# Six stores in place of four for the rows of a 96-slot expert job

## The reference, cut to what matters

```
for e in range(N_EXP):
    out = out + combine[..., e:e + 1] * swiglu(h, w_gate[e], w_up[e], w_down[e])
h = h + out
return rms_norm(h, final_norm)
```

## Time and profile before

| | |
|---|---|
| median of three runs | 1287.35 us (1285.57 to 1287.72) |
| the profiled execution's own time | 1288.18 us |
| its span, first to last instruction | 1286.3 us |
| PE busy | 1225.8 us (95%) |
| DVE, ACT, POOL busy | 354.1, 298.1, 54.5 us |
| mean granted TensorE clock | 0.978 of full speed |
| DMA moved | 433.32 MB, mean 337 GB/s |

### The profile page before, as it was taken

One profiled execution on the slowest core, in us unless ns is written; L12 is line 12 of the kernel. 1 busy time (PEld: TensorE's weight loads), 2 busy tenths in 40 slices (PEclk: granted clock), 3 DMA queues, 4 the chain that ended last, 5 costly groups with the idle time before them and its releaser, 6 DMA issues.

```text
span 1286.3 us, 23777 instructions
## 1 busy us (share of the span) xinstructions
PE 1225.8 (95%) x10720; PEld 671.6 (52%) x10720; DVE 354.1 (28%) x758; ACT 298.1 (23%) x539; POOL 54.5 (4%) x99
## 2 busy tenths in 40 slices
PE   9999999999999999999999999999999989999827
PEld 9888888888887634234334233533443423443213
DVE  6787655557578501001001000100100100110013
ACT  7575644335566300000000000000000000000011
POOL 2012000000220300000000000000000000000010
PEclk9999999999999999999998999999999999999858
DMA  9534965545522999999999999999999999999980
GB/s 344 200 99 135 317 232 182 179 163 199 193 91 70 409 433 427 432 429 428 428 430 430 430 431 429 430 427 430 428 387 427 432 427 433 428 427 429 430 364 34
DMA packets 55045, 433.32 MB, mean 337 GB/s; under 512 B 3758, under 2 KB 8544, under 8 KB 41888
## 3 DMA queue, kind: packets, MB, share of 16 engines
q1 hardware_dynamic: 50416, 420.92, 79.7%
q0 software_dynamic: 2768, 8.52, 2.2%
q10 hardware_dynamic: 1760, 2.36, 0.5%
HBM read 423.26 MB, written 8.52 MB: 336 GB/s over the span
## 4 chain that ended last, share of the span: by engine, by line
PE 79%; DMA 14%; another core or an unknown queue 4%; DVE 2%; ACT 0%; issue 0%; SPq 0%; DVEq 0%; ACTq 0%
PE bank L2527 44%; PE bank L1900 9%; PE bank L1905 8%; PE bank L1901 8%; DMA ring<-in_od_w_gate_e_dram 6%; DMA aside<-in_od_w_gate_e_dram 3%; DMA ring<-in_od_w_down_e_dram 3%; DMA ring<-in_od_w_up_e_dram 2%; PE bank L2504 2%; PE bank L2616 1%; PE bank L2096 1%; PE bank L2177 1%; PE bank L2168 1%; PE bank L2367 0%; PE bank L2153 0%
## 5 line engine op out<-in xcount | busy, mean ns | idle before, releaser
L2527 PE MATMUL bank<-ring,xg 128*32 128x448 f32 x4128 | 398.8, 546 | 14.3 <-DMA ring<-in_od_w_up_e_dram 10.1
L2527 PEld LDWEIGHTS bank<-ring,xg 128*32 128x32 f32 x4128 | 133.5, 111 | 276.8 <-issue 254.5
L2527 PE MATMUL bank<-ring,m_ht 128*32 128x512 f32 (+1 forms) x2520 | 212.1, 497 | 7.8 <-DMA ring<-in_od_w_down_e_dram 7.8
L1819 DVE TENSOR_TENSOR m_hh<-m_hh,bank 128x896 f32<-128x896 f32 x20 | 21.7, 1087 | 619.1 <-PE bank L2527 618.9
L2527 PEld LDWEIGHTS bank<-ring,m_ht 128*32 128x32 f32 x2520 | 82.7, 111 | 133.5 <-issue 95.2
L1900 PE MATMUL bank<-w_hi,xt_hi 128*128 128x512 f32 (+3 forms) x384 | 147.1, 387 | 0.0
L1901 PE MATMUL bank<-w_hi,xt_lo 128*128 128x512 f32 (+3 forms) x384 | 142.9, 377 | 0.0
L1154 DVE TENSOR_TENSOR w_lo<-raw,w_hi 128x2048 fp32r<-128x2048 f32 (+4 forms) x52 | 114.6, 2211 | 44.2 <-ACT w_hi L556 43.2
L556 ACT ACTIVATE w_hi<-raw 128x2048 fp32r<-128x2048 f32 (+4 forms) x52 | 96.6, 1863 | 73.6 <-PE bank L1905 73.3
L2527 PE MATMUL bank<-aside,xg 128*32 128x448 f32 x992 | 97.1, 547 | 2.8 <-DMA aside<-in_od_w_up_e_dram 2.3
L1905 PE MATMUL bank<-w_lo,xt_hi 128*128 128x512 f32 (+3 forms) x384 | 91.9, 378 | 0.1
(11 more groups left out here) (358 smaller groups left out, 984.8 us busy)
## 6 DMA issues: line engine op xcount, KB each, us to landing
ring<-in_od_w_up_e_dram SPq DMA_DIRECT2D x26, 3584.0 KB, 25.3
ring<-in_od_w_down_e_dram SPq DMA_DIRECT2D x26, 3584.0 KB, 31.6
ring<-in_od_w_gate_e_dram SPq DMA_DIRECT2D x22, 3584.0 KB, 25.1
aside<-in_od_w_up_e_dram SPq DMA_DIRECT2D x6, 3584.0 KB, 25.1
aside<-in_od_w_gate_e_dram SPq DMA_DIRECT2D x6, 3584.0 KB, 32.8
aside<-in_od_w_down_e_dram SPq DMA_DIRECT2D x5, 3584.0 KB, 30.9
ring<-in_od_w_gate_e_dram SPq DMA_DIRECT2D x8, 1792.0 KB, 10.1
raw<-in_od_w_qkv_dram SPq DMA_DIRECT2D x12, 1024.0 KB, 5.1
```

What stands on the lines that cost most here:

```text
L1819: dve.tensor_tensor(halves(k), halves(k), both(up_bank(k)), ALU.mult).then_inc(m_h[k], 1)
L2527: return pe.matmul(B[bank][32 * g:32 * g + 32, c0:c0 + w.shape[-1]], tokens, w, start=first, stop=last, tile_position=(0, 32 * g))
```

## The change

A 96-slot job stores rows 0 to 31 and rows 64 to 95 by one store for each group of 32 partitions, four in place of two. So such a job has six stores, a 64-slot job still has four. The stores no longer add the same number to `y_stored`; `stores_before` gives how much the jobs before add, and the waits and the starting value follow from it. The wait of line 950, the release of the read-back and all other code stay as they were. (`big_before(j)` counts the 96-slot jobs before job j.)

```diff
+def stores_before(j):
+
+    return 96 * big_before(j) + 64 * (j - big_before(j)) if isinstance(j, int) else 96 * j - 32 * (len(SMALL_JOBS) - 1)
...
                 if last:
-                    act.wait_ge(y_stored, j * 64 + 64)
+                    act.wait_ge(y_stored, stores_before(j) + 96)
                     act.activation(stat[:, 92:93], ones[:, 0:1], ACT.Copy).then_inc(rows_all_stored, 1)
...
             def leave(j, thirds=ALL_THIRDS):
 
-                act.wait_ge(y_stored, j * 64 + 64)
+                act.wait_ge(y_stored, stores_before(j) + 96)
...
                     act.dma_start(to[:, 0:512], y[0:96, 0:512]).then_inc(y_stored, 16)
                     act.dma_start(to[32:64, 512:], y[96:P, 0:512]).then_inc(y_stored, 16)
-                    for k in range(2):
-                        act.dma_start(to[64 * k:64 * k + 32, 512:].rearrange("r (h f) -> h r f", h=2),
-                                      y[64 * k:64 * k + 64, 512:768]).then_inc(y_stored, 16)
+                    for g in range(4):
+                        r, c0 = 64 * (g // 2), 512 + 256 * (g % 2)
+                        act.dma_start(to[r:r + 32, c0:c0 + 256], y[32 * g:32 * g + 32, 512:768]).then_inc(y_stored, 16)
...
             dve.engine_nop().then_inc(y_out, 2)
-            dve.engine_nop().then_inc(y_stored, 64)
+            dve.engine_nop().then_inc(y_stored, 96)
```

## The result

The changed kernel takes 1271.79 us (median of four runs, 1270.73 to 1272.41) against 1287.32 us before: a ratio of 0.9877, 95% interval 0.9865 to 0.9889, 15.5 us less. The profiled execution took 1272.29 us at a span of 1270.5 us and a mean granted clock of 0.986. Some lines carry new numbers: the wait's activation is L956 (it was L951), the product L1824 (L1819), the matmuls of `across` and `down` L2532 (L2527), the additions L1805 (L1800), the new stores L990.

The account below looks back on a forecast made before the run. Weight traffic was taken to be at its DMA limit, with job 6's late stores stopping TensorE 24.2 us at the end. `down` ending 17.7 us earlier takes 1288.18 to 1270.5 profiled, 1270 median; range 1264 to 1275.

Parts of the forecast that it names:

- Two engines: Line 984's two old stores in 96-slot jobs: each runs on 2 DMA engines; with the change the queue's packets become 2000.
- Landing at 1193: Job 6's new stores: 22 packets per engine land at 1193 (1191 to 1201); ScalarE's wait falls from 51.1 to some 3 us.
- Two more issues: ScalarE issuing four stores instead of two: at most 3.6 us against 1.79, covered before the next silu, cost 0.
- Earlier jobs worth nothing: Faster stores in 96-slot jobs before job 6: worth 0, with 0 to 2.1 us kept for the range.
- Coalescing: Rule against small transfers: two more stores, at a fixed 2.0 us each, land 4 us later, still covered before `across` ends.
- The read-back: Read-back of stored rows, moved into the weight traffic: from 1197 to 1241, delaying the last weights by 5.3 us.
- The end of `down`: Last matmuls, held twice by weights: end at 1257.3 (1256.4 to 1258.1) against 1274.98, 17.7 us less.
- The sum: Whole kernel: 1288.18 - 17.7 = 1270.5 us for the profiled execution, 1269.7 for the median, stated as 1270.
- A: Rival: the read-back finds gaps, weights come in time, `down` ends at 1252.1; 22.9 us earlier, 1264.5 us; chance 8%.
- B: Rival: 1 KB rows, not the pattern, make the stores slow, so four take as long as two; 1287.4 us; chance 5%.
- C: Rival: longer waits keep TensorE's clock low through the last pairs and `down`, 24.1 us becoming 48.2; 1292 us; chance 3%.

Follow-up runs that it names:

- run with two outermost: Changed kernel, but the first store of a 96-slot job (2 KB rows) gets a DRAM-side pattern with an outermost dimension of two: 1282.6 us in one run.
- the changed kernel's other profile: The changed kernel run again without alteration, beside three kernels that begin the read-back later: 1271.46 us, ratio 0.9881.
- run with job 6 alone: Kernel before with the four new stores in job 6 only; jobs 1, 3 and 4 keep the two old stores: 1271.34 us, ratio 0.9871.
- run with jobs 1, 3 and 4 alone: Kernel before with the four new stores in jobs 1, 3 and 4 only; job 6 keeps the two old stores: 1286.15 us, ratio 0.9990.
- run with ten stores: Changed kernel with the four new stores of a 96-slot job cut into eight of 512 B rows: 1271.77 us, ratio 0.9877.
- exponential first: Kernel before, slow stores kept; in the last job ScalarE does the exponential ahead of its wait for the stores: 1272.12 us, ratio 0.9879.

## Why the prediction was right, point by point

*Two engines.* Right, and shown both ways: 2000 packets in the queue as forecast, and two outermost makes 2 KB rows slow as well. By the Trainium skill, "DMA: Bandwidth & Descriptors", section "Why a DMA increments its semaphore by 16 and not by 1", the number of engines follows from the slowest dimension of both sides. The completions of all three patterns, 2, 4 and 16 to a store, agree.

*Landing at 1193.* The activation of line 956 started at 1192.89. With 1 us a packet and 5 us to begin, 22, 34 and 40 packets gave 1193, 1205 and 1211 (from an issue at 1165.8); measured are 1192.89, 1205.24 and 1209.49 (issue at 1164.69, so 1209.7 by the rule). The run with two outermost puts 64 packets on each of its two engines: from its issue at 1167.65 that makes 1236.65, and 1236.63 was measured. The rule has its limit in the kernel before: 76 packets from 1165.79 would make 1246.8, and the stores landed at 1240.78, 6 us sooner. The 5 us and the 1 us are fitted to these runs and don't hold for every queue.

*Two more issues.* 2.64 us for four in place of 1.79 for two (1.75 in the changed kernel's other profile); the next silu starts at 1187.25 as before. Cost 0.

*Earlier jobs worth nothing.* The run with job 6 alone has the whole gain. The run with jobs 1, 3 and 4 alone doesn't prove the nought: its interval just touches 1, and something up to 2.4 us, about the 2.1 that the range had kept for it, stays possible.

*Coalescing.* The Trainium skill's page "DMA: Bandwidth & Descriptors", section "Rules for kernel authors", says to put small transfers together. Here, in the run with ten stores, the transfers are smaller still and cost only turns in the queue: 12.35 us of landing time for 12 more packets per engine (1192.89 to 1205.24), and no time. That is 3.1 us for each of four more stores, not the 2.0 that the prediction had taken from the Trainium skill. The section on the anatomy of one DMA, on the same page of the Trainium skill, gives that figure for DMAs that GpSimd issues, and these are ScalarE's. The wait was covered: it ended 16.5 us before VectorE's product began (1221.77).

*The read-back.* Taken at 5.3 us; the intervals show 5.1, and 5.3 in the changed kernel's other profile (five intervals of 47.9 us in all, from 1197.37 to 1245.24). It lasted until 1239.23, when the additions begin, and they were covered. The forecast said 1241, but its own terms, 36 packets of 1.16 us from 1197, make 1238.8.

*The end of `down`.* Forecast 1257.3, within 1256.4 to 1258.1; measured 1259.09. This is the term that was mis-sized, by 1.8 us. TensorE waited three times for `down` weights, not twice (0.69, 3.54 and 2.27 us). The landings forecast at 1225.8, 1235.4 and 1244.4 were 1227.15, 1236.94 and 1245.45, 1.1 to 1.5 us late. Most of that was there before the read-back stretched the pairs: the pair of 1196.59 in the execution of before came at 1197.76, 8.44 us after the one ahead of it (1189.32). It looks like a spread between executions: with the old stores in job 6 the same start is 1196.59, 1197.36 (jobs 1, 3, 4 only) and 1198.03 (exponential first), with the new ones 1197.76, 1197.37 (again) and 1196.86 (job 6 only). The two sets lie over each other.

The rest, 0.7 us, is the last two quarters: 13.6 us where 12.0 to 13.7 was counted and a middle of 12.9 taken. The clock fell after the wait of 2.27 us and came back (columns as for the stretches above):

```profile
1245.45:1249.00 3.55, 3.55 (x36) 1.70 (x40) 0.00 (x0) 0.00 (x0) 0.00 (x0) 0.53 0.86 353
1249.00:1252.00 3.00, 3.00 (x62) 1.68 (x56) 0.00 (x0) 0.00 (x0) 0.00 (x0) 1.00 0.47 194
```

The prediction tied such a fall to the length of the wait, by two rows. The runs don't bear that out: in the changed kernel's other profile a pair after a wait of 2.29 us took 6.22 us, the fast value; after 3.54 us the clock stayed up (the quarter at 1236.94 took 6.25 us); and in the run with job 6 only the last two quarters came after a wait of 2.43 us, had a clock of 1.00 and took 12.29 us. What decides it is open; it is worth 1.4 to 1.7 us, and the forecast took about half of it.

The last weights landed at 1254.0 to 1254.5; forecast were 1251.1 to 1253.5, with 1252.9 used in the sum: again the shift of some 1.1 us. The weight queue from 1254 to 1256, the last packets before the output:

```profile
q1 hardware_dynamic: 2, 0.00, 0.5%
```

*The sum.* 1270.5 for the profiled execution, 1272.29 measured; 1270 for the median, 1271.79 measured. Mechanism and path were right; the 1.8 us are the end of `down`.

*The rivals.* A (no DMA limit) is out: `down` has three DMA waits, and even with the read-back out of the way (exponential first) it ended at 1254.30 and not at 1252.1. B (stores stay slow) is out by ScalarE's wait of 3.2 us. C (the clock stays low) is out: 0.99 from 1222 to 1246, and a dip of 3.5 us behind it. C's break-even at nine tenths of `down` also leaves out the 4 us that it charged to `across`, with which it is nearer eight tenths. What the prediction didn't see is that the order in ScalarE's program alone would have given the same time: behind the wait stood the exponential, and that order was how the slow stores stopped TensorE.

## What to carry to other kernels

Count the completions of a store in its queue: here they told on how many engines it ran, and a pattern with two outermost was slow with rows of 1 KB and of 2 KB. Then ask what stands behind the wait for it on the waiting engine; here an exponential of 0.2 us (1.5 with the table load in front of it) held the last product for 24 us, and moving it or speeding the stores gave the same time. And when a wait of 24 us goes, look for the resource that was already full beside it: of the 24.2 us, 15.5 came back as time, mostly since the weights and the read-back needed the same DMA engines.

## What was not expected of the hardware

While two queues were busy side by side, they moved about one packet each in turn, whatever the sizes. In the run with ten stores, from 1171 to 1205.2 us, ScalarE's queue moved 521 packets of 0.35 MB in all and the weight queue 556 of 14.25 MB:

```profile
q1 hardware_dynamic: 556, 14.25, 96.6%
q10 hardware_dynamic: 521, 0.35, 3.2%
```

For the read-back in the changed kernel, from 1198 to 1239 us, it is 576 to 606. That the two alternate one for one on each engine is the simplest reading of these counts; no view shows the order itself. So a store's time went by its packets per engine and not by its bytes, near 1 us for a row of 512 B, of 1 KB or of 2 KB alike: 22 packets landed by 1193, 34 by 1205, and, at 0.92 us each, the 65 that two engines still had after 1181 in the kernel before by 1240.8. It isn't the packet's own time: at the end, with no weights in flight, each output store of 512 KB, 9 packets per engine, landed 2.8 us after its issue. The 36 packets per engine of the read-back, 32 of them of 4 KB, delayed the weights by only 0.14 us each (5.1 / 36) while they took 1.2 us each themselves (1197 to 1239).
